# Latent attention mixer: order of the pair turn, the sample's turn and division, and the mask product

## The reference, cut to what matters

```python
for a, e in _q_blocks(q_nope.shape[1]):            # blocks of 128 queries
    nk = min(tk, ((q_off + e - 1) // CHUNK + 1) * CHUNK)
    s = (einsum('bqhd,bkhd->bhqk', q_nope[:, a:e], k_nope[:, :nk])
         + einsum('bqhr,bkr->bhqk', q_rope[:, a:e], k_rope[:, :nk])) * C_SCALE
    vis = (arange(nk)[None, :] // CHUNK) <= (tq[:, None] // CHUNK)     # CHUNK = 64
    p = softmax(where(vis, s, -inf), axis=-1)
    outs.append(einsum('bhqk,bkhd->bqhd', p, v[:, :nk]))
```

## Time and profile before

| what | value |
|---|---|
| median of 3 runs | 1871.65 us (1871.32 to 1871.89) |
| profiled execution, its own time | 1868.09 us |
| span of the profile, first to last instruction | 1866.3 us |
| TensorE matmuls busy | 1799.6 us, 96% |
| VectorE busy | 1149.0 us, 62% |
| ScalarE busy | 864.8 us, 46% |
| mean granted TensorE clock | 0.991 of 2.4 GHz |

### The profile page before, as it was taken

How to read it: one execution, slowest core, us unless ns; L and a number is a source line. 1 busy time by engine, 2 the same in 40 slices (tenths; PEclk the granted TensorE clock), 3 DMA queues, 4 the chain that set the end, 5 groups by cost and what they waited for, 6 DMA issues and landing times.

```text
span 1866.3 us, 34719 instructions
## 1 busy us (share of the span) xinstructions
PE 1799.6 (96%) x13562; PEld 1670.5 (90%) x13562; DVE 1149.0 (62%) x1843; ACT 864.8 (46%) x1454; POOL 179.2 (10%) x123
## 2 busy tenths in 40 slices
PE   5999999999999999999999999999999999999995
PEld 4999855999999989999987799999999855999995
DVE  4886557666556545664566675555886557666553
ACT  2655422455444375554444555444655422455432
POOL 2000023110011001100120020011000123110011
PEclk9999999999999999999999999999999999999998
DMA  4565423555555624555533155555565423555541
GB/s 134 152 168 169 142 85 119 182 158 160 169 167 158 199 72 128 160 165 170 163 110 117 46 154 166 166 169 158 158 166 168 140 91 125 187 154 168 169 161 57
DMA packets 155869, 272.98 MB, mean 146 GB/s; under 512 B 22677, under 2 KB 28258, under 8 KB 155754
## 3 DMA queue, kind: packets, MB, share of 16 engines
q1 hardware_dynamic: 155754, 271.37, 46.6%
HBM read 250.55 MB, written 20.78 MB: 145 GB/s over the span
## 4 chain that ended last, share of the span: by engine, by line
PE 88%; DVE 7%; ACT 3%; issue 1%; SPq 1%; POOL 1%; DMA 0%; POOLq 0%; ACTq 0%; DVEq 0%
PE PS L1632 86%; PE PS L1637 2%; DVE WLO L986 1%; ACT PB L887 1%; SPq L356 1%; DVE HL L1270 1%; DVE C L1219 0%; DVE XGL L1005 0%; DVE TMP L1516 0%; POOL SQ L1560 0%; ACT TMP L938 0%; DVE KG L1183 0%; DVE NT L1011 0%; DVE NV L1017 0%; DVE NT L1012 0%
## 5 line engine op out<-in xcount | busy, mean ns | idle before, releaser
L986 DVE TENSOR_TENSOR WLO<-RAWT,WHI 128x512 fp32r<-128x512 f32 (+1 forms) x904 | 644.3, 730 | 492.0 <-ACT WHI L628 490.0
L628 ACT ACTIVATE WHI<-RAWT 128x512 fp32r<-128x512 f32 (+1 forms) x904 | 554.4, 626 | 656.0 <-PE PS L1632 655.4
L1632 PE MATMUL PS<-XGH,WHI 128*128 128x288 f32 x1776 | 528.5, 298 | 16.1 <-DVE WLO L986 15.9
L1632 PE MATMUL PS<-HH,WHI 128*128 128x288 f32 (+1 forms) x1792 | 529.5, 295 | 4.0 <-issue 4.0
L1632 PE MATMUL PS<-HH,WLO 128*128 128x288 f32 (+1 forms) x1792 | 530.2, 296 | 0.0
L1632 PE MATMUL PS<-HL,WHI 128*128 128x288 f32 (+1 forms) x1792 | 529.2, 295 | 0.0
L1632 PE MATMUL PS<-XGH,WLO 128*128 128x288 f32 x1776 | 526.3, 296 | 0.0
L1632 PE MATMUL PS<-XGL,WHI 128*128 128x288 f32 x1776 | 525.4, 296 | 0.0
L1632 PEld LDWEIGHTS PS<-XGH,WHI 128*128 128x128 f32 x1776 | 334.5, 188 | 21.6 <-DVE WLO L986 14.5
L1632 PEld LDWEIGHTS PS<-HH,WHI 128*128 128x128 f32 x1792 | 337.3, 188 | 6.8 <-issue 5.9
L1632 PEld LDWEIGHTS PS<-HL,WHI 128*128 128x128 f32 x1792 | 337.4, 188 | 0.0
(11 more groups left out here) (332 smaller groups left out, 1448.7 us busy)
## 6 DMA issues: line engine op xcount, KB each, us to landing
RAWT<-in_w_ff_dram SPq DMA_DIRECT2D x256, 512.0 KB, 3.7
RAWT<-in_a_w_up_dram SPq DMA_DIRECT2D x64, 512.0 KB, 3.8
RAWT<-in_a_w_down_dram SPq DMA_DIRECT2D x32, 512.0 KB, 3.7
RAWT<-in_b_w_qkv_dram SPq DMA_DIRECT2D x24, 512.0 KB, 3.8
RAWT<-in_a_w_q_dram SPq DMA_DIRECT2D x16, 512.0 KB, 3.7
RAWT<-in_a_w_k_dram SPq DMA_DIRECT2D x16, 512.0 KB, 3.8
RAWT<-in_a_w_v_dram SPq DMA_DIRECT2D x16, 512.0 KB, 3.7
C<-in_state_mlstm_C_dram SPq DMA_DIRECT2D x8, 1024.0 KB, 5.7
```

The source lines that it names most:

```text
L628: act.activation(hi, raw, ACT.Copy).then_inc(weight_hi, 1)
L986: dve.tensor_tensor(lo, raw, hi, ALU.subtract).then_inc(weight_lo, 1)
L1632: return pe.matmul(out, lhsT, rhs, start=start, stop=stop, **kw)
```

## The change

On TensorE, turn(s - 2) stands ahead of sample_turn(s // 2 - 1) in an even step, and in `mla_scores` the mask's two products stand ahead of the eight others (they now start the accumulation, and the last positional product ends it). On ScalarE the PTB copy stands ahead of the two CPTS copies. On VectorE the sample's division of group g moves from the end of the odd step 2g + 1 to the next even step, behind top(s) and ahead of normed(s - 1).

```diff
@@ ScalarE, mla_mix @@
+                    p = s - 2
+                    if 0 <= p < CH // 2:
+                        act.wait_ge(c_xp, p + 1)
+                        act.activation(PTB[:, p % 2, 0, :], PS[:, 5, 0:384], ACT.Copy).then_inc(c_pt0, 1)
                     if s >= 2 and s % 2 == 0 and s <= CH // 2:
                         g = s // 2 - 1
                         act.wait_ge(ss_xp, g + 1)
                         act.activation(CPTS[:, g % 2, 0, :], PS[:, 6, 160:288], ACT.Copy)
                         act.activation(CPTS[0:TS, g % 2, 1, :], PS[0:TS, 6, 288:416], ACT.Copy).then_inc(ss_pt, 1)
-                    p = s - 2
-                    if 0 <= p < CH // 2:
-                        act.wait_ge(c_xp, p + 1)
-                        act.activation(PTB[:, p % 2, 0, :], PS[:, 5, 0:384], ACT.Copy).then_inc(c_pt0, 1)
@@ VectorE, mla_mix @@
                     if s < CH // 2:
                         top(s)
+                    if s % 2 == 0 and s <= CH // 2:
+                        dve.wait_ge(ss_exp, g)
+                        link(dve.reciprocal(CSTS[:, 3:4], CSTS[:, 2:3]))
+                        dve.tensor_scalar(CPS[:], CPS[:], CSTS[:, 3:4], None, ALU.mult).then_inc(ss_nrm, 1)
...
-                    if sample:
-                        dve.wait_ge(ss_exp, g + 1)
-                        link(dve.reciprocal(CSTS[:, 3:4], CSTS[:, 2:3]))
-                        dve.tensor_scalar(CPS[:], CPS[:], CSTS[:, 3:4], None, ALU.mult).then_inc(ss_nrm, 1)
@@ TensorE, mla_scores @@
+                for a in range(2):
+                    diag = PS[:, b0 + a, :].rearrange("p (d c) -> p d c", d=2)[:, :, 0:P]
+                    mm(diag, IDENR[:], MSKR[:].unsqueeze(1).to_broadcast([P, 2, P]), True, False, skip_group_check=True)
                 for c, n, q0 in ((0, 128, 0), (128, 256, 128)):
                     for a in range(2):
                         r = slice(64 * a, 64 * a + 64)
-                        mm(PS[:, b0 + a, c:c + n], QN[r, p, q0:q0 + P], KN[r, p, 0:n], c == 0, False,
+                        mm(PS[:, b0 + a, c:c + n], QN[r, p, q0:q0 + P], KN[r, p, 0:n], False, False,
                            skip_group_check=True)
...
-                        mm(PS[:, b0 + a, c:c + n], QR[r, g, q0:q0 + P], KR[r, 0:n], False, False,
-                           skip_group_check=True)
-                for a in range(2):
-                    diag = PS[:, b0 + a, :].rearrange("p (d c) -> p d c", d=2)[:, :, 0:P]
-                    ins = mm(diag, IDENR[:], MSKR[:].unsqueeze(1).to_broadcast([P, 2, P]), False, True,
-                             skip_group_check=True)
+                        ins = mm(PS[:, b0 + a, c:c + n], QR[r, g, q0:q0 + P], KR[r, 0:n], False, True,
+                                 skip_group_check=True)
@@ TensorE, mla_mix @@
+                    if s >= 2:
+                        turn(s - 2)
                     if s % 2 == 0:
                         sample_turn(s // 2 - 1)
-                    if s >= 2:
-                        turn(s - 2)
                     if s >= 3:
                         outputs(s - 3)
```

## The result

The changed kernel takes 1877.01 us (median of 8 runs, 1872.88 to 1878.92), the kernel before 1871.77 (8 runs, 1870.97 to 1873.08): a ratio of 1.0027, 95% interval 1.0018 to 1.0036. It is 5.2 us slower by the medians. I had said 1873.0 and a range of 1869.0 to 1875.8.

What follows compares the result with a forecast made beforehand. TensorE, busy for 96% of the span, was taken as the bound, so time is won only where it idles or is slowed. The reordering's -0.82 us plus one clock fall gave +1.35: 1871.65 + 1.35 = 1873.0 us, range 1869.0 to 1875.8.

Steps and rivals of the forecast that it cites:

- The walk: Pair loop, from each VectorE maximum (top) to the next and to the output projection: -0.82 us if the clock keeps.
- Part 1: Division behind the next top on VectorE: top(2) no longer waits, interval 1 to 2 falls from 4.24 to 2.75 us.
- Part 2: Pair turn ahead of the sample's: even steps 5.32 us instead of 4.68, 0.64 lost twice; 2 to 3 gains 0.95.
- the end: From top 7 to the projection's start: 8.81 us before, a loss of 0.34.
- The idles: TensorE waits ahead of the sample turns of steps 2, 4, 6, and two waits in step 8, 1.5 ahead of turn(6).
- Part 3: Mask product first in the scores: taken as 0 us, bounds -1.4 to +1.4 from exposed weight loads.
- the load at the head: Identity weight load for the mask product: by the skill's rule alone, hidden once per step, sum nearer its lower bound.
- one fall: Half clock from about 1033.5, behind step 4's 2.2 us idle: +0.7 or +2.2 in sum, +1.35 taken; chance 0.52.
- rival B: A second clock fall in the last step, slowing the projection: +3.0 to +4.8 us, 1874.7 to 1876.4; chance 0.12.
- the 1060: Output projection on TensorE: a start before 1054 or after 1060 would show the prediction wrong.
- A: Rival: the clock keeps despite step 4's 2.2 us idle, -0.82 us, 1870.8 us; chance 0.28.
- C: Rival: faster through mask savings or runs losing a fall elsewhere, -2.2 to -4 us, 1867.6 to 1869.4; chance 0.08.

Runs made afterwards that it cites:

- first_only: Kernel before with the new order for group 0 alone, the mask product in its old place: 1869.25 us, ratio 0.9994.
- after_hold: Changed kernel with unread mask products filling TensorE's idles ahead of the sample turns of steps 2, 4, 6 and ahead of turn(6): 1871.37 us, ratio 1.0003.
- mask_only: Kernel before with the mask product first and nothing else changed: 1870.79 us, ratio 1.0005.
- after_outputs_first: Changed kernel with outputs(s-3) ahead of the sample turn in even steps: 1868.58 us, ratio 0.9991.
- after_hold8: Changed kernel with 12 unread mask products ahead of turn(6) in step 8 alone: 1876.75 us, ratio 1.0039.
- turn_only: Kernel before with the pair turn ahead of the sample turn on TensorE and PTB ahead of CPTS on ScalarE: 1868.56 us, ratio 0.9989.
- early_splits: Kernel before with the weight splits moved from step 3 to ScalarE's step 0 and VectorE's step 1: 1870.88 us, ratio 1.0004.
- division_only: Kernel before with only the sample's division moved behind the next top on VectorE: 1875.64 us, ratio 1.0024.
- before_hold: Kernel before with unread mask products ahead of the sample turns of step 2 (12) and step 8 (18): 1870.09 us, ratio 1.0004.
- first_only_hold: first_only with unread mask products in the idles of step 2 (7) and step 8 (18): 1868.84 us, ratio 0.9993.
- best: first_only_hold with the weight splits moved from step 3 to ScalarE's step 0 and VectorE's step 1: 1864.41 us, ratio 0.9974.
- after_hold4: Changed kernel with 17 unread mask products in the idle of step 4 alone: 1870.37 us, ratio 0.9999.

## Why the prediction was wrong

**The walk was right.** Part 1: top(2) at 2.58 behind top(1), where I had 2.75; first_only, with the mask's old place, has 2.76. Part 2: even steps at full clock are 5.44 and 5.43 long in after_hold, against my 5.32; the end is 9.22 against 9.15. The sum is -0.64 against my -0.82. The idles came out at 1.07, 2.30, 0.93, 1.60 and 0.31, where I had 0.9, 2.2, 0.9, 1.5 and 0.4.

**Part 3 was nearly right**: 0 by the median of mask_only and by blocks of 2.14 us behind outputs. One block is a little shorter. In the changed kernel the scores of pair 1, behind the products that make the values, take 1015.51 to 1017.54 = 2.03 us, against 1015.35 to 1017.50 = 2.15 before (timeline of TensorE, after, then before):

```profile
1015.51 0.40 PE L1632 MATMUL PS<-MSKR,IDENR 128*128 128x256 f32 x2
...
1017.54 0.48 PE L1632 MATMUL PS<-KN,QN 64*32 64x160 f32 x8
```

```profile
1015.35 0.93 PE L1632 MATMUL PS<-KN,QN 64*128 64x128 f32 x8
...
1017.50 0.48 PE L1632 MATMUL PS<-KN,QN 64*32 64x160 f32 x8
```

So 0.12 us is gained in this block, 0.02 in the one behind the sample's first turn (1022.63 to 1024.75, 2.12 us), and nothing behind the outputs; the bound of 1.4 us for all seven was far off. Why the one block gains is not shown. The Trainium skill (TensorE: Matmul & The Clock Gate, step-by-step section) lets a weight load be pulled ahead where the row groups don't conflict, or where it goes into the background weight buffer. The mask's load takes all 128 rows and shares rows with what runs before it in either case, so the first condition doesn't tell the two blocks apart, and it gave no ground for my sentence that the load at the head could be hidden in every step. Of the second no row here shows anything.

**The step that failed is the clock's: the length of the half clock behind the idle of step 4.** I priced one fall at 3.4 to 6.7 us of half clock, 1.5 to 3.0 us of time, and took 2.2, nearly the middle. What the profile shows is some 10 us of it, for 4.7 us of time. Taken against the walk's 5.32, 4.87 and 5.32, tops 4 to 5, 5 to 6 and 6 to 7 took 2.2, 2.4 and 0.1 us more. The price for each us of half clock was right (1.5 for 3.4, 3.0 for 6.7, 4.7 for 10); the length was not. And the second fall came too, to which I had given only 0.12. It cost 1.2 us at the end (10.37 against 9.15), less than the 1.7 to 3.4 that I had for it. Sum: -0.82 + 4.7 + 1.2 = 5.1, where the loop lost 5.0. So the mechanism of the forecast and of rival B held, and the size of the first term did not. The lengths on record, 3.4 and 6.7, were draws and not ends, and I used the longest as a bound. The range ended at 1875.8, inside B's own span of 1874.7 to 1876.4, and the measured 1877.0 is beyond both. The projection's start, 1061.73, is past the 1060 that I had named as a sign of being wrong.

**The evidence for the falls was read too narrowly.** The profile of before holds more idles than I named. The idle of 1.98 us has a twin at 1583.18 with no fall, and one of 1.81 ahead of 957.28 was followed by 3.4 us of half clock. Those of 1.0 to 1.2 us outside the stage are six and not five, since one at 52.80 belongs with them. And at 231.4 the clock fell for 3.4 us though no idle longer than 0.63 us stood ahead of it:

```profile
232.00:233.00 1.00, 1.00 (x28) 1.00 (x22) 0.39 (x1) 0.96 (x2) 0.91 (x1) 0.50 0.06 16
```

So the length of an idle tells the risk of a fall and not the fall.

**A rule on idle gaps.** In the loop's profiles of all these kernels, before and after among them, stand 19 idles of 1.3 to 3.1 us; behind or in 12 of them the clock fell, behind 7 it did not. The Trainium skill (TensorE: Matmul & The Clock Gate, section HAM oscillation) warns only of idle gaps longer than any of these, so by its rule none of them should have slowed the clock. The measurement decides.

**Rivals.** A, that the clock keeps, fell: none of the eight runs is below 1872.88, where A said 1870.8. It was a real possibility, since idles of 2.11 to 2.73 us had no fall in other profiles. C fell for this change. In after_outputs_first the next scores still stand behind the sample turn, but with the outputs ahead of it their path is no longer the longest (tops 4.70 apart), and that kernel came out faster than before.

## What to carry to other kernels

An idle engine time has two prices: its own length and the clock that falls behind it; in this loop the second was 5.6 us where the reordering by itself moved 0.6. When a short operation is put behind another on one engine, look for who waits for it on TensorE and what is queued behind that wait: here pair outputs and the next scores, which had no need of it. Move it only where its old place really stopped the engine (the first of four groups), and use what becomes free (the splits). Filling an idle with unread products saved 5.6 us of the loop where there was a long fall to avoid, and nothing measurable in the kernel before.

## What the runs showed of the hardware

The half clock isn't left as soon as TensorE is busy again. In after_hold8 TensorE was busy for 16.65 of 17 us of scores, turns and outputs and stayed at 1.2 GHz; in other runs of the same loop it returned after 3.4 us (turn_only), 6.7 (before) or 10 (after).

Of eleven idles of 0.93 to 1.17 us in the loops of all profiles none had a fall in the 4 us behind it; in turn_only one came behind an idle of 1.32 us, 4 us after one of 1.01. Idles of 2.46 to 2.48 us at the same place of step 8 had no fall in three profiles (before, mask_only, early_splits) and one in first_only. In division_only the clock fell 0.9 us into an idle of 3.09.

With 6 to 18 unread products in the long idles the clock was 1.00 in the loop of each of the four kernels that filled all of them (after_hold, before_hold, first_only_hold, best). After_outputs_first had 1.00 as well with an unfilled idle of 2.11, so one such profile by itself proves nothing; the medians of after_hold and after_hold4 against that of the change do.
